# A streaming encoder step: weight slots released by the projections' own semaphore, products of ones ahead of the first projection, the last token tile scaled on ScalarE, and the mLSTM gate rows turned in two blocks

## What is computed

```
xn = x * rsqrt(mean(x*x) + EPS) * norm_mix
u, q, k, v, o, ig, fg, g_s5, g_ml = split(dot(xn, w_in))
y_s5 = glu(gelu(s5_scan(u)))                     # S5 branch
h    = scan(mlstm_chunk, q, k, v, ig, fg)        # mLSTM branch, 5 chunks
mix  = sigmoid(g_s5) * y_s5 + sigmoid(g_ml) * dot(sigmoid(o) * norm(h), w_ml_out)
x    = x + dot(mix, w_out)
x    = x + moe(rmsnorm(x))                       # top 4 of 32, clamped SwiGLU
y    = rmsnorm(x)
```

## Time and profile before

| | |
|---|---|
| median of 3 runs | 1257.6 us (1257.39 to 1258.66) |
| profiled execution | 1258.4 us, span 1256.7 us |
| PE busy / weight loads | 1221.8 / 552.6 us |
| DVE / ACT / POOL busy | 472.6 / 174.7 / 246.2 us |
| DMA | 440.31 MB, mean 350 GB/s over the span |
| first expert product (L949) | 327.01 us from the start |
| chain that ended last | PE 69%, DMA 25%, DVE 4% |

### The profile page before, as it was taken

How to read it: one execution, slowest core, us unless ns; L and a number is a source line. 1 busy time by engine, 2 the same in 40 slices (tenths; PEclk the granted TensorE clock), 3 DMA queues, 4 the chain that set the end, 5 groups by cost and what they waited for, 6 DMA issues and landing times.

```text
span 1256.7 us, 21374 instructions
## 1 busy us (share of the span) xinstructions
PE 1221.8 (97%) x7763; PEld 552.6 (44%) x7764; DVE 472.6 (38%) x914; ACT 174.7 (14%) x311; POOL 246.2 (20%) x438
## 2 busy tenths in 40 slices
PE   7999999999999999999999999999999999999997
PEld 5666666678543333333333333333333333333332
DVE  6689767234532222222332222222232222222223
ACT  4652015115300000000000000000000000000002
POOL 2078760000112111111112111111111211111100
PEclk9999999999999999999999999999999999999999
DMA  8323332659899999999999999999999999999994
GB/s 230 101 67 102 101 101 69 188 194 384 314 409 428 426 430 428 427 431 427 427 432 426 427 432 426 428 431 426 428 431 426 430 429 427 429 429 427 429 429 190
DMA packets 69352, 440.31 MB, mean 350 GB/s; under 512 B 13024, under 2 KB 42376, under 8 KB 44744
## 3 DMA queue, kind: packets, MB, share of 16 engines
q1 hardware_dynamic: 66952, 438.72, 85.1%
q10 hardware_dynamic: 2368, 1.15, 0.3%
HBM read 437.39 MB, written 1.87 MB: 350 GB/s over the span
## 4 chain that ended last, share of the span: by engine, by line
PE 69%; DMA 25%; DVE 4%; issue 1%; ACT 0%; DVEq 0%; POOL 0%; SPq 0%; ACTq 0%; POOLq 0%
DMA big<-in_w_gate_up_dram 25%; PE psum L949 24%; PE psum L525 13%; PE psum L992 13%; PE psum L929 5%; PE psum L915 4%; PE psum L503 3%; PE psum L816 3%; PE psum L537 1%; PE psum L958 1%; PE psum L979 1%; PE psum L639 0%; PE psum L656 0%; DVE acc L1878 0%; DVE m L1597 0%
## 5 line engine op out<-in xcount | busy, mean ns | idle before, releaser
L949 PE MATMUL psum<-big,m 128*64 128x512 f32 x2048 | 472.2, 597 | 9.8 <-DMA big<-in_w_gate_up_dram 9.8
L1834 DVE TENSOR_TENSOR acc<-acc,psum 128x512 f32<-128x512 f32 (+1 forms) x192 | 123.1, 681 | 577.8 <-PE psum L929 575.5
L949 PEld LDWEIGHTS psum<-big,m 128*64 128x64 f32 x2048 | 137.0, 136 | 315.6 <-issue 254.3
L992 PE MATMUL psum<-big,m 128*64 128x512 f32 x1024 | 226.8, 595 | 0.0
L525 PE MATMUL psum<-big,m 128*128 128x320 f32 x576 | 164.0, 440 | 3.0 <-PE psum L525 1.5
L1391 POOL COPY m<-uT 96x64 bf16 x32 | 7.4, 233 | 659.0 <-PE psum L979 658.4
L525 PEld LDWEIGHTS psum<-big,m 128*128 128x128 f32 x576 | 108.1, 192 | 52.8 <-issue 12.2
L992 PEld LDWEIGHTS psum<-big,m 128*64 128x64 f32 x1024 | 70.7, 137 | 134.1 <-issue 127.9
L929 PE MATMUL psum<-m 64*128 64x512 f32 (+1 forms) x384 | 106.7, 632 | 0.0
L1274 ACT ACTIVATE m<-m 128x512 f32<-128x512 f32 x32 | 20.2, 631 | 554.8 <-DVE m L1851 554.8
L1400 POOL TENSOR_SCALAR m<-cst,m 128x128 f32<-128x128 f32 x96 | 74.8, 788 | 7.7 <-POOL m L1395 7.7
(11 more groups left out here) (295 smaller groups left out, 851.2 us busy)
## 6 DMA issues: line engine op xcount, KB each, us to landing
big<-in_w_gate_up_dram SPq DMA_DIRECT2D x128, 2048.0 KB, 29.0
big<-in_w_down_dram SPq DMA_DIRECT2D x64, 2048.0 KB, 30.8
m<-in_w_in_dram SPq DMA_DIRECT2D x18, 1024.0 KB, 6.6
m<-in_w_s_glu_dram SPq DMA_DIRECT2D x8, 512.0 KB, 4.6
m<-in_w_out_dram SPq DMA_DIRECT2D x3, 1024.0 KB, 5.5
acc<-in_x_prompt_dram SPq DMA_DIRECT2D x4, 512.0 KB, 5.2
m<-in_w_ml_out_dram SPq DMA_DIRECT2D x2, 1024.0 KB, 5.0
big<-in_w_out_dram SPq DMA_DIRECT2D x1, 1024.0 KB, 7.7
```

The costliest lines, as they stand in the source:

```text
L949: mm = pe.matmul(psum[SLOT * hf:SLOT * hf + SLOT, GB + gu, :], xeT[:, GU_CHUNKS * k + c, :], big[:, base:base + 512], start=(c + k == 0), ...
L992: mm = pe.matmul(psum[SLOT * hf:SLOT * hf + SLOT, DB, :], hT[:, m, c, :], big[:, base:base + 512], start=False, stop=(c == DN_CHUNKS - 1 a ...
L1834: v.tensor_tensor(x, x, psum[0:n, CB + hf, :], ALU.add).then_inc(S("added"), 1)
```

## The change

Six edits:

1. `group_used` goes. SP waits for `pj_done` itself, at the number of the last projection that reads the slot (`last_use`), and POOL for `pj_done` 72 in place of `group_used` 25.
2. DVE first sets a 128x128 tile `busy` to one; PE multiplies it by itself in bank 1: 14 products before the first transposes, 2, 3 and 3 after the transposes of the three tiles (`FILL`).
3. The last token tile is scaled by ACT instead of DVE, after DVE's reciprocal.
4. DVE's order is: the first half of tile 0's columns, the reciprocal of tile 2, the second half, tile 1, tile 2.
5. `row_columns` stands in two blocks, after projections 12 and 13, instead of one after 16; its copies on ACT are a step of their own at 13.
6. Waits follow: `row_columns` waits for `dm_read` 2 instead of `y_read` 1, and the first `s5_out` for `cols_ready` (bank 7 is used by both).

```
+        busy = w.take(P)
...
+        def last_use(g):
+            if g < G_GLU:
+                return 15 if g in (6, 7) else 2 * g + 1
+            return T_GLU + 4 * (g - G_GLU) + 3
...
+        FILL = (14, 2, 3, 3)
...
-                        (4, "gate_abs"), (4, "softplus"), (5, "state_in"), (6, "gate_scan"), (7, "row_factors"), (16, "row_columns")):
+                        (4, "gate_abs"), (4, "softplus"), (5, "state_in"), (6, "gate_scan"), (7, "row_factors"), (13, "row_copies")):
             plan[j].append((step, 0))
+        for n, j in enumerate((12, 12, 13, 13)):
+            plan[j].append(("row_columns", n))
...
                 if g >= 3:
-                    sp.wait_ge(S("group_used"), g - 2)
+                    sp.wait_ge(S("pj_done"), last_use(g - 3) + 1)
...
-            def row_columns(_):
-                pe.wait_ge(S("rows_ready"), 1)
-                pe.wait_ge(S("y_read"), 1)
-                for n, k in enumerate((R_WI, R_WE, R_M)):
+            def row_columns(n):
+                if n == 0:
+                    pe.wait_ge(S("rows_ready"), 1)
+                    pe.wait_ge(S("dm_read"), 2)
+                if n < 3:
+                    k = (R_WI, R_WE, R_M)[n]
...
                 if t == 0:
-                    pe.wait_ge(S("dm_read"), 2)
+                    pe.wait_ge(S("cols_ready"), 1)
                 else:
                     pe.wait_ge(S("y_read"), t)
-                if t == 1:
-                    pe.wait_ge(S("cols_ready"), 1)
...
+            def fill(n):
+                for _ in range(FILL[n]):
+                    pe.matmul(psum[:, 1, 0:P], busy, busy, start=True, stop=True)
+
+            pe.wait_ge(S("busy_set"), 1)
+            fill(0)
             pe.wait_ge(S("filled"), 2)
             for i, (t0, n) in enumerate(TILES):
...
+                fill(i + 1)
...
-                if j == 15:
-                    group_used(j, 2)
-                elif j % 2 == 1 and j != 13:
-                    group_used(j)
...
+            act.wait_ge(S("inv_last"), 1)
+            s64 = slice(0, TS)
+            nc.scalar.activation(xn[s64, 2, :], acc[s64, 2, :], ACT.Copy, scale=st[s64, 11:12]).then_inc(S("xn_ready"), 1)
...
-            pool.wait_ge(S("group_used"), 25)
+            pool.wait_ge(S("pj_done"), T_OUT + 12)
...
-            for i in range(3):
+            for i in range(2):
                 scaled(i)
...
+            columns(0, 0, 4)
+            inverse_rms(2, TS, 0)
+            dve.sem_inc(S("inv_last"), 1)
+            columns(0, 4, DK)
+            columns(1, 0, DK)
+            columns(2, 0, DK)
```

More of the change, by code:

```diff
@@ L539, in project_v @@
                 mm.then_inc(S("pj_done"), 1)
-            def group_used(j, n=1):
-                pe.wait_ge(S("pj_done"), j + 1)
-                pe.sem_inc(S("group_used"), n)
             def s5_columns(_):
@@ L606, in row_columns @@
                                       start=True, stop=True, skip_group_check=True)
+                    return
                 for h in range(H):
@@ L786, in _ @@
                 project(j, G_GLU + i // 4, 4, uT, (i % 4 // 2) * P + (i % 2) * 256)
-                if i % 4 == 3:
-                    group_used(j)
                 for step, n in plan[j]:
@@ L866, in _ @@
             rows_out(2, 3)
-            group_used(T_OUT + 11)
             pe.wait_ge(S("mask_ready"), 2)
@@ L1100, in row_factors, with row_copies @@
                 nc.scalar.activation(rows[R_WE], rows[R_WE], ACT.Exp).then_inc(S("rows_ready"), 1)
-            def row_columns(_):
+            def row_copies(_):
                 act.wait_ge(S("cols_mm"), 1)
@@ L1146, in _ @@
                          c_matrix=c_matrix, b_matrix=b_matrix,
-                         row_factors=row_factors, row_columns=row_columns, decay_exp=decay_exp, natural=natural,
+                         row_factors=row_factors, row_copies=row_copies, decay_exp=decay_exp, natural=natural,
                          group_root=group_root, states_out=states_out, s5_last=s5_last, s5_out_states=s5_out_states)
@@ L1421, in scaled, with columns @@
                 v.tensor_scalar(xn[0:n, i, :], acc[0:n, i, :], inv, None, ALU.mult).then_inc(S("xn_ready"), 1)
+            def columns(i, k0, k1):
+                t0, n = TILES[i]
+                dve.wait_ge(S("xT"), i + 1)
+                src = cut(flat(psum[:, 2 + 2 * i:4 + 2 * i, :]), DK, P)[:, k0:k1, 0:n]
+                ins = v.tensor_tensor(xnT[:, k0:k1, t0:t0 + n], src, vc[:, k0:k1][:, :, None].to_broadcast([P, k1 - k0, n]), ALU.mult)
+                if k1 == DK:
+                    ins.then_inc(S("xnT_ready"), 1)
+                else:
+                    do.start(ins)
+            v.memset(busy, 1.0).then_inc(S("busy_set"), 1)
             v.memset(st[:, 13:14], EPS).then_inc(S("eps_set"), 1)
-            for i in range(3):
+            for i in range(2):
                 scaled(i)
```

## The result

| | before | after |
|---|---|---|
| median | 1258.13 us (4 runs, 1257.39 to 1258.73) | 1249.45 us (4 runs, 1247.77 to 1250.33) |
| ratio | | 0.9921, 95% interval 0.9900 to 0.9942 |
| profiled execution | 1258.4 us, span 1256.7 | 1250.33 us, span 1248.6 |
| first projection | 13.00 | 11.98 |
| first expert product | 327.01 | 318.83 |

The change is faster by 8.7 us in the medians and 8.1 us between the two profiled executions. I had said 1246.7 (1243.8 to 1250.9). "Faster" is a small effect here, 0.8% of the run, but the interval of the ratio is clear of 1.

A forecast was written before the change was run, and what follows sets the result against it. Bound: the experts' weight stream, whose start waits for PE's front. Terms -0.95 + 0.05 - 1.8 - 8.2 = -10.9 took the profiled 1258.4 us to 1247.5, as a median 1246.7; range 1243.8 to 1250.9.

The forecast's parts named there:

- its two terms of 1.4 and 0.6: Lower end of the forecast: waits of projections 7, 9 and 33 pay too, 1.4 us; runs differ by 0.6 us.
- rival A: Start: the clock stays down or falls again in a gap before the projections; 1249.0 us, chance 0.12.
- Rival B: S5 branch becomes the bound, so waits removed between 80 and 182 us buy nothing; 1250.4 us, chance 0.12.
- The bound: Expert stage: the stream of weights, 29.35 us an expert, sets the end; time off the front comes off one for one.
- Term 1: Start: reordered DVE columns and ACT's scaling let the first projection start at 12.05 instead of 13.00; -0.95 us.
- Term 2: Start: products of ones raise PE's clock before the transposes; first two projections 8.85 instead of 10.65 us; -1.8 us.
- Term 3: Front: removing 24 waits in PE's queue, each of which lets PE run empty; -8.2 us.
- Term 4: Gate rows' products moved earlier on PE; DVE falls back some 1.8 us and catches up; 0 us.
- Its signs: For the gate rows: DVE's start after `s5_in(8)` later than PE, no such delay at `s5_out`.
- C: Expert stage: the stream does not move up with the front, or only partly; 1256 to 1257 us, chance 0.05.
- D: Expert stage: the fuller front costs TensorE's clock or the stream's rate, making it slower; 1260.8 us, chance 0.03.

The follow-up runs named there:

- the control: The changed kernel plus one register operation per block of experts, holding the loop's end at zero or above; 1249.21 us, ratio 0.9925.
- w1: The changed kernel with the 24 waits for pj_done put back in TensorE's queue at the old places; 1254.17 us.
- s1: The changed kernel with VectorE again scaling all three tiles first, then making the columns tile by tile, the ones kept; 1250.57 us.
- n2: The changed kernel with its 22 products of ones one column wide instead of 128, at the same places; 1252.43 us.
- o1: The changed kernel with only the 14 products of ones ahead of the transposes, without the 2, 3 and 3 between them; 1251.30 us.
- w2: The changed kernel with the 24 waits put back in TensorE's queue and a semaphore increment behind each; 1257.88 us.
- r1: The changed kernel with the gate rows' products and copies back behind projection 16, with the waits of before; 1249.99 us.

## Why the prediction was right

The direction, the bound and the terms held; the sum did not quite. By itself my forecast ran from 1244.5 to 1248.5 (its two terms of 1.4 and 0.6 give 1244.7 at the lower end), and the measured 1249.45 lies above that. It is inside the stated range because that was stretched to 1250.9 for rivals A and B, and neither took place. That much is luck.

1. **The bound.** Right. From first to last product of the expert stage it is 921.6 us before, 921.8 after, 921.8 in the control and 921.7 in w1: the stream of weights moves with the front, one for one, as the 29.35 us between loads had said.
2. **Term 1, the start (-0.95).** Right as a size (13.00 to 11.98, s1 back at 13.05), but costed to the path's end without its next neighbour. I followed DVE and ACT, and not the DMA that lands behind projection 2. The gate weights took back 0.8 us of terms 1 and 2 in the profiled execution. The row was there to be read: before, SyncE's queue issued the second half of the gate weights at 21.79 us, TensorE used them at 28.75 without a wait, and I was moving that use 3 us forward.
3. **Term 2, the clock (-1.8).** Right: 8.85 us, the weight loads fast from the first. What I had wrong is the size of what the ones do together. Without wide ones the transposes are slow and the start is 1.5 us late too, where rival A had allowed 0.5 for it (n2: +3.2 us in all, by the medians), and the blocks between the transposes, costed at nothing, are what keeps the clock up (o1: +2.1). So the -0.95 of term 1 hangs on term 2. Rival A, that the clock falls again in a gap, did not happen in the change and did in o1.
4. **Term 3, the waits (-8.2).** Right for what was removed: w2 gives it back, +8.67 in the times, 7.8 in the traces. The reason was half right: I spoke of the wait alone, and 3.7 of it hung on the increment behind it. The estimated 3.1 us by the fixed part of a lone matmul in the Trainium skill (TensorE: Matmul & The Clock Gate, "Single matmul latency") is too small against 5.0 for the waits alone.
5. **Term 4 (0).** Right, r1: 0.07 us. Its signs are there too: DVE waits 4.84 us for PE at `s5_in(4)` instead of 2.25, and its first read of `s5_in(8)` starts at 116.10 as before, now behind its own work and not behind PE.
6. **What is missing.** 10.9 us forecast, 8.2 in the trace. The step that failed is the sum's silent last term: that the freed front stays at full clock. The stretch at 1.2 GHz at 74 us costs 1.7, the gate weights 0.8; 0.2 is left over. With the stretch absent (the control's profile) 10.3 of the 10.9 are there. The forecast lay 2.8 us under the median: 2.2 by a gain of 8.7 instead of 10.9, and 0.5 because I took the kernel before at 1257.6 and its four runs gave 1258.13. The two causes are of that size, though how many of the executions behind the median had the slow stretch isn't known; only profiled ones show it.

None of the rivals took place. C and D are excluded by the 921.6 and 921.8 us of point 1. Rival B, the S5 branch, is excluded by the trace: no `s5_out` waits, and the first product behind GpSimd's last step starts at 178.06 instead of 182.61.

## What to carry to other kernels

A wait for one's own result in a full queue, with the increment behind it, costs more than the wait's row shows (0.54 against 0.30 us here), and the increment has a good part of it (0.33 and 0.21); let the consumer wait on the producer's own semaphore. When a front gets shorter, list the DMAs that land just behind each moved step before you add up the gain. And read the instruction queue's packets in every profile: a kernel with a large loop can lose 50 us by a few instructions taken out ahead of it, and an experiment that removes instructions must be made against one that replaces them by small ones.

## What the runs showed of the hardware that I had not expected

- How many instructions stand ahead of a large loop in TensorE's code can decide whether the loop is refetched: 22 products fewer (88 instructions by the profile's count) made 84 packets of 21, 14 stalls of up to 4.1 us, and 1305 us of 1249. The same products behind the loop changed nothing.
- The clock falls for a stretch of 3 to 7 us in a queue that never stands still: TensorE is busy 100% of 70 to 77 us in the profile after, with 22 products of four rows (44 records) ahead of the fall. It happens in some executions and not in others (8 of the 12 profiles with both decay matrices in one piece), and one stretch costs 1.7 us where the runs of a kernel lie 2 to 4 us apart. What sets it off is open.
- Short gaps in a row at the start can lose the clock again (o1: 0.80, 0.36, 1.02 and 0.83 us; granted clock 0.50 from 12 to 16 us, projections 11.81 us instead of 8.85), while one gap of 1.20 us did not (s1: 8.85).
- An increment of a semaphore in TensorE's queue, behind a wait, costs 0.21 us between two projections (w2 against w1, at three places; over all 24 it is 3.7 us in the medians, 0.15 each).
